# A twelve-unit ring for the expert weights, half of it over the front's dead temporaries, and a loop over pairs of items

## The reference, cut to what matters

```python
x = x + merged @ w_out[l]                       # end of the two attention branches
x = x + moe_ffn(rms_norm(x, ffn_norm_g[l]), router_w[l], router_b[l],
                w_gate_up[l], b_gate_up[l], w_down[l], b_down[l])
return rms_norm(x, final_norm_g)
...
top_logit, top_e = lax.top_k(logits, TOP_K)     # 4 of 32 experts for each token
gate = jax.nn.softmax(top_logit, axis=-1)
...
gu = xb @ w_gu[e] + b_gu[e]                     # 1024 x 2048 weights per expert
glu = jnp.minimum(gu[:, :D_FF], SWIGLU_LIMIT)
lin = jnp.clip(gu[:, D_FF:], -SWIGLU_LIMIT, SWIGLU_LIMIT)
act = glu * jax.nn.sigmoid(SWIGLU_ALPHA * glu) * (lin + 1.0)
return act @ w_d[e] + b_d[e]                    # 1024 x 1024 weights per expert
```

## Time and profile before

| | |
|---|---|
| median of 3 runs | 1183.23 us (1181.96 to 1184.37) |
| profiled execution, its own time | 1181.82 us |
| its span | 1180.0 us |
| granted TensorE clock, mean | 0.995 |
| TensorE busy | 1102.3 us, 93% |
| VectorE, ScalarE, GpSimd busy | 279.0, 164.0, 10.2 us |
| moved by DMA | 431.22 MB, 365 GB/s over the span |

### The profile page before, as it was taken

How to read it: one execution, slowest core, us unless ns; L and a number is a source line. 1 busy time by engine, 2 the same in 40 slices (tenths; PEclk the granted TensorE clock), 3 DMA queues, 4 the chain that set the end, 5 groups by cost and what they waited for, 6 DMA issues and landing times.

```text
span 1180.0 us, 13249 instructions
## 1 busy us (share of the span) xinstructions
PE 1102.3 (93%) x5094; PEld 473.9 (40%) x5094; DVE 279.0 (24%) x662; ACT 164.0 (14%) x341; POOL 10.2 (1%) x28
## 2 busy tenths in 40 slices
PE   7999999999999999999999999999999999999996
PEld 5578887633333333333333333333333333333332
DVE  2056432321111211111111111111111111111113
ACT  2144440210001000000000000000000000000002
POOL 0101000000000000000000000000000000000000
PEclk9999999999999999999999999999999999999998
DMA  9823313469999999999999999999999999999993
GB/s 307 315 75 147 136 72 126 160 288 405 429 429 430 427 427 430 429 428 427 429 429 429 427 427 430 429 428 427 429 429 430 427 427 430 429 428 427 429 429 158
DMA packets 43265, 431.22 MB, mean 365 GB/s; under 512 B 5808, under 2 KB 7984, under 8 KB 18640
## 3 DMA queue, kind: packets, MB, share of 16 engines
q1 hardware_dynamic: 42960, 430.46, 87.2%
q10 hardware_dynamic: 288, 0.52, 0.1%
HBM read 429.92 MB, written 1.05 MB: 365 GB/s over the span
## 4 chain that ended last, share of the span: by engine, by line
DMA 57%; PE 41%; DVE 1%; issue 1%; ACT 1%; SPq 0%; DVEq 0%; ACTq 0%
DMA raw<-in_w_gate_up 56%; PE bank L835 15%; PE bank L493 8%; PE bank L526 4%; PE bank L851 4%; PE bank L718 2%; PE bank L497 2%; PE bank L535 1%; PE bank L672 1%; PE bank L770 1%; PE bank L803 1%; DMA x_res<-in_x 1%; PE bank L736 0%; PE bank L813 0%; DVE x_res L1457 0%
## 5 line engine op out<-in xcount | busy, mean ns | idle before, releaser
L835 PE MATMUL bank<-raw,xT 128*64 128x512 f32 x2048 | 465.2, 598 | 56.0 <-DMA raw<-in_w_gate_up 54.4
L835 PEld LDWEIGHTS bank<-raw,xT 128*64 128x64 f32 x2048 | 137.9, 136 | 357.7 <-issue 230.7
L851 PE MATMUL bank<-raw,actT 128*64 128x512 f32 x1024 | 233.2, 597 | 0.0
L1408 DVE COPY ev_gu<-bank 128x512 f32<-128x512 f32 x32 | 22.1, 692 | 532.7 <-PE bank L835 532.7
L851 PEld LDWEIGHTS bank<-raw,actT 128*64 128x64 f32 x1024 | 71.7, 137 | 132.5 <-issue 126.7
L1401 DVE TENSOR_TENSOR gub<-bank,bias_gu 128x512 f32<-128x512 f32 x64 | 43.9, 686 | 169.5 <-PE bank L497 169.5
L1065 ACT COPY ev_gu<-bank 128x512 f32<-128x512 f32 x32 | 18.8, 586 | 413.3 <-PE bank L835 413.3
L803 PE MATMUL bank<-ev_dn,scat 64*128 64x512 f32 x256 | 64.3, 621 | 1.2 <-ACT ev_dn L1075 0.8
L770 PE MATMUL bank<-x_res,onehot 128*64 128x512 f32 x264 | 62.3, 592 | 0.0
L493 PE MATMUL bank<-hT,raw 128*128 128x256 f32 x256 | 58.9, 383 | 0.0
L493 PEld LDWEIGHTS bank<-hT,raw 128*128 128x128 f32 x256 | 47.5, 190 | 8.4 <-issue 2.5
(11 more groups left out here) (234 smaller groups left out, 594.1 us busy)
## 6 DMA issues: line engine op xcount, KB each, us to landing
raw<-in_w_gate_up SPq DMA_DIRECT2D x128, 2048.0 KB, 25.4
raw<-in_w_down SPq DMA_DIRECT2D x64, 2048.0 KB, 24.9
raw<-in_w_in SPq DMA_DIRECT2D x6, 2048.0 KB, 14.5
raw<-in_w_out SPq DMA_DIRECT2D x2, 2048.0 KB, 9.7
raw<-in_w_branch_mla SPq DMA_DIRECT2D x1, 2048.0 KB, 9.0
raw<-in_w_branch_dsa SPq DMA_DIRECT2D x1, 2048.0 KB, 7.8
raw<-in_w_in SPq DMA_DIRECT2D x1, 1664.0 KB, 16.8
x_res<-in_x SPq DMA_DIRECT2D x2, 512.0 KB, 4.9
```

Of the source, the lines that this page charges most:

```text
L835: mm = pe.matmul(GU[pair][half * SLOTS:(half + 1) * SLOTS, :], xT[:, c, b, :], w[:, at:at + BLK], start=u == 0 and k == 0, stop=last and k ...
L851: mm = pe.matmul(DN[half * SLOTS:(half + 1) * SLOTS, :], actT[:, c, u, :], w[:, at:at + BLK], start=u == 0 and c == 0, stop=u == DN_UNITS ...
L1408: dve.tensor_copy(ev_gu[:, 1, :], GU[1][:, :]).then_inc(lin_ev, 1)
```

## The change

The ring gets twelve slots (`SLOTS_W`). Six of them are those of the front, now called `front_raw`; the other six lie over the front's temporaries, which are laid out anew in six groups of 16 KB per partition. The expert units go round the twelve slots in the order `ORDER`, which begins with the slots whose contents are dead first. The first twelve units are issued one by one, each behind a wait for the last reader or writer of what lies there; from the thirteenth on the waits are on `used` again, twelve units back. Since twelve units are two items, the loops of SyncE and TensorE go over pairs of items (`pairs`); those of ScalarE and VectorE still go over items.

```diff
+SLOTS_W = 2 * UNITS
+ORDER = (6, 7, 1, 8, 2, 3, 4, 9, 10, 5, 0, 11)
...
-        raw = sb("raw", [P, RING, UNIT])
-        n_items = sb("n_items", [P, 1], I32)
+        n_items = sb("n_items", [P, 2], I32)
...
+        front_raw = fb("front_raw", [P, RING, UNIT])
...
+        raw = sb("raw", [P, SLOTS_W, UNIT])
-        ev_x = sb("ev_x", [P, BLK])
-        ev_dn = sb("ev_dn", [P, BLK])
+        ev = sb("ev", [P, BLK])
-        sig = sb("sig", [P, BLK])
-        scat = sb("scat", [P, TOKENS])
+        glu, lin, sig = gub[:, 0], gub[:, 1], ev_gu[:, 0]
+        scat = gated[:, :, :].rearrange("p t n -> p (t n)")
+        final_g = raw[:, ORDER[0], 0:D]
...
+        def landed_expert(eng, j, place):
+            slot = ORDER[place % SLOTS_W]
+            eng.wait_ge(raw_in[slot], 16 * j + (16 * (place // SLOTS_W + 1) + arrived(slot)))
+            return raw[:, slot, :]
...
@@ SyncE @@
-            sp.dma_start(cst[:, :], consts).then_inc(cst_in, 16)
+            sp.dma_start(cst[:, :], consts[:, 0:KEPT]).then_inc(cst_in, 16)
...
+            sp.dma_start(cst2[:, 0:sum(CONST.values()) - KEPT], consts[:, KEPT:]).then_inc(cst2_in, 16)
...
+            sp.wait_ge(ml_rot, 1)
+            load_gate_up(0, 0, ORDER[0])
+            sp.wait_ge(s_mx, 7)
+            sp.wait_ge(pv_ps, 6)
+            load_gate_up(0, 1, ORDER[1])
+            used_up(sp, 7)
+            load_gate_up(0, 2, ORDER[2])
+            sp.wait_ge(s_mx, 12)
+            load_gate_up(0, 3, ORDER[3])
+            used_up(sp, 8)
+            load_gate_up(1, 0, ORDER[4])
+            used_up(sp, 9)
+            load_gate_up(1, 1, ORDER[5])
+            used_up(sp, 10)
+            load_gate_up(1, 2, ORDER[6])
+            load_gate_up(1, 3, ORDER[7])
+            sp.wait_ge(br_ok, 2 * KC)
+            load_down(0, 0, ORDER[8])
+            used_up(sp, 11)
+            load_down(0, 1, ORDER[9])
+            used_up(sp, 12)
+            load_gate_up(2, 0, ORDER[10])
+            sp.wait_ge(lg_ps, 2)
+            load_gate_up(2, 1, ORDER[11])
...
+                def load(k, start, e, u):
+                    sp.wait_ge(used, SLOTS_W * j + (k + 1 - SLOTS_W))
+                    start(e, u, ORDER[k])
+                load(0, load_gate_up, even, 2)
+                load(1, load_gate_up, even, 3)
...
+            sp.wait_ge(used, SLOTS_W * pairs + (1 - SLOTS_W))
+            for n in range(2):
+                sp.dma_start(final_g[:, n * BLK:(n + 1) * BLK],
+                             final_norm_g[n * BLK:(n + 1) * BLK].partition_broadcast(P)).then_inc(final_in, 16)
@@ TensorE @@
-            with pe.Fori(2, items) as i:
-                gate_up(i, 0)
+            with pe.Fori(1, pairs) as j:
+                for odd in range(2):
+                    i = 2 * j + odd
+                    gate_up(j, odd, 0)
...
@@ ScalarE @@
             def glu_out(i):
                 act.wait_ge(glu_ps, i + 1)
+                if not isinstance(i, int) or i > 0:
+                    act.wait_ge(act_ok, i)
...
-            act.wait_ge(sums_ok, 1)
-            for j in range(2):
-                act.dma_start(gain[:, j * BLK:(j + 1) * BLK], ...
@@ VectorE @@
+            dve.wait_ge(cst2_in, 16)
...
+            dve.tensor_scalar(n_items[:, 0:1], r_s[:, 0, 0:1], float(EXPERTS - 2), None, ALU.add)
+            dve.tensor_scalar(n_items[:, 1:2], r_s[:, 0, 0:1], 0.5, float(EXPERTS // 2 - 2), ALU.mult, ALU.add).then_inc(n_ok, 1)
...
+            weigh_tokens(0)
             with dve.Fori(2, items) as i:
-                weigh_tokens(i - 2)
                 next_tokens(i)
                 activate(i)
                 product(i)
+                dve.wait_ge(scat_ps, 2 * i - 2)
+                weigh_tokens(i - 1)
@@ the program @@
-    nc = _bacc.Bacc("TRN2", target_bir_lowering=False, num_devices=1)
+    nc = _bacc.Bacc("TRN2", target_bir_lowering=False, num_devices=1, dynamic_dma_scratch_size=1024)
```

More of the change, by code:

```diff
@@ L62 @@
 GATES_ATT = (0, 1, 2, 3, 4, 5, 6, 7, 8, 9, 10)
-CONST = {"ident": P, "before": P, "ones": P, "slot": P, "causal": P, "invfreq": ROPE // 2}
+CONST = {"ident": P, "ones": P, "slot": P, "before": P, "causal": P, "invfreq": ROPE // 2}
 CONST_AT = {}
@@ L68 @@
     CONST_AT[_name] = sum(CONST[k] for k in CONST_AT)
+KEPT = CONST_AT["before"]
 def constants():
@@ L212, in build @@
         bd_in = sem("bd_in")
-        sums_ok = sem("sums_ok")
         final_in = sem("final_in")
-        raw_in = [sem(f"raw_in{i}") for i in range(RING)]
+        raw_in = [sem(f"raw_in{i}") for i in range(SLOTS_W)]
         out_done = sem("out_done")
@@ L467, in _ @@
-            sp.wait_ge(n_ok, 1)
-            items = sp.value_load(n_items[0:1, 0:1], min_val=EXPERTS - 2, max_val=EXPERTS * CHUNKS - 2) + 2
-            with sp.Fori(2, items) as i:
-                e = sp.snap(i % EXPERTS)
-                e_last = sp.snap((i + (EXPERTS - 1)) % EXPERTS)
-                for u in range(UNITS):
-                    sp.wait_ge(used, UNITS * i + (u + GU_UNITS - UNITS - RING + 1))
-                    if u < GU_UNITS:
-                        load_gate_up(e, u, slot_of(GU_UNITS + u))
-                    else:
-                        load_down(e_last, u - GU_UNITS, slot_of(GU_UNITS + u))
@@ L478, in _ @@
-            for u in range(DN_UNITS):
-                sp.wait_ge(used, UNITS * items + (u + GU_UNITS - UNITS - RING + 1))
-                load_down(EXPERTS - 1, u, slot_of(GU_UNITS + u))
+            sp.wait_ge(ml_rot, 1)
[7 more added lines that the diff above has]
+            load_gate_up(0, 3, ORDER[3])
@@ L802, in scatter @@
                         rows = slice(half * SLOTS, (half + 1) * SLOTS)
-                        mm = pe.matmul(ACC[2 * t + half][:, :], scat[rows, t * P:(t + 1) * P], ev_dn[rows, :],
+                        mm = pe.matmul(ACC[2 * t + half][:, :], scat[rows, t * P:(t + 1) * P], ev[rows, :],
                                        start=False, stop=True, skip_group_check=True)
@@ L839, in gate_up, with down @@
                 mm.then_inc(used, 1)
-            def down(i, u, place):
+            def down(j, odd, u, last=False):
+                i = 2 * j + odd
                 pe.wait_ge(act_ok, i + 1)
@@ L845, in down @@
                     pe.wait_ge(dn_ev, i)
-                landed_expert(pe, i + 1, place)
-                w = raw[:, slot_of(GU_UNITS + place), :]
+                w = landed_expert(pe, j, UNITS * odd + (GU_UNITS if last else UNITS + GU_UNITS - DN_UNITS) + u)
                 for c in range(4):
@@ L900, in _ @@
             scatter(items - 2)
-            down(items - 1, 0, 0)
+            down(pairs - 1, 1, 0, last=True)
             turn_scatter(items - 1)
-            down(items - 1, 1, 1)
+            down(pairs - 1, 1, 1, last=True)
             scatter(items - 1)
```

201 lines of the change are left out of this document (97 added, 104 removed).

## The result

The changed kernel takes 1148.88 us (median of 4 runs, 1144.81 to 1149.92), the kernel before 1183.8 us (median of 4, 1181.96 to 1187.07). The ratio is 0.9699, with a 95% interval of 0.9671 to 0.9727. The forecast was 1153.9 us with a range of 1151.0 to 1158.5 us: the direction and most of the size are right, and the time lies 2.1 us under the range. The profiled execution has a span of 1148.1 us against 1180.0 us.

What follows compares the result with a forecast made beforehand. Weight transfers were taken to bound the last stage, TensorE the stages before. Execution 1181.82 us less 29.4 us for six units' lead, other terms nothing, gives 1152.5; 1.4 us up to the median makes 1153.9 us, range 1151 to 1158.5.

Steps and rivals of the forecast that it cites:

- 4.894 us a unit: Last stage: time of one expert unit's transfer, at six units per 29.365 us item, in both kernels.
- the lead: Last stage: twelve slots put loads six units further ahead, so every arrival comes 29.4 us earlier.
- D. A deeper queue moves more per us: Rival on the weight stream: more transfers in flight raise the rate to 435 GB/s, giving 1141 us; 2%.
- The floor: Item loop: TensorE's free run ends at 1077.7 us, leaving 38.2 us of slack; transfers still bind from near 680 us.
- The end of item 31's gate and up matmuls: Sign near the loop's end: this point moves from 1145.29 us to near 1116 us.
- The twelve early issues: Front: twelve expert units issued ahead of 231.3 us as their slots come free, the last landed by 238 us.
- Shared buffers: Item loop: added waits on VectorE and ScalarE for merged buffers cost nothing, with 1.3 us per item as cover.
- The end: After the last item: the scatter matrix's wait and the later load of final gains cost nothing, with 4 us of cover.
- The start: Front: splitting the constants costs or gains at most 0.5 us, taken as 0.
- A, fewer units ahead: Rival on the loads: each unit too late to keep the queue full costs 4.9 us, 1158.8 us for one; 5%.
- B, code fetched at each jump: Rival in TensorE's loop: the doubled body is fetched anew, fifteen jumps at 4.8 us, giving 1188 us; 4%.
- C: Rival on the bound: transfers are hidden anyway and TensorE is the true bound, so time stays at 1183; 1%.

Runs made afterwards that it cites:

- e3_after_off_256: The changed kernel with 192 bytes of padding ahead of the ring, so its slots begin 192 past a multiple of 256: 1153.07 us, ratio 0.9733.
- six ahead: The changed kernel with its first twelve units loaded early, but later loads held to six units ahead of the one in use: 1172.89 us, ratio 0.9911.
- nine ahead: The changed kernel with its first twelve units loaded early, but later loads held to nine units ahead of the one in use: 1163.94 us, ratio 0.9821.
- half units: The changed kernel with each expert unit loaded and released in two halves of 1 MB, in rows of 8 KB: 1151.6 us, ratio 0.9723.
- kernel before on 256: The kernel before with 64 bytes of padding ahead of its ring, so its slots begin at a multiple of 256 bytes: 1177.96 us, ratio 0.9946.

## Why the prediction was wrong

Its mechanism was right and one term was mis-sized: **"4.894 us a unit", taken over for the changed kernel.** The prediction priced the lead (six units by 4.894 us, 29.4 us) and left the pitch of the stream at "29.365" in the last stage; a unit of the changed kernel took 4.863 us. The lead measured 29.3 us at the old place of the ring and 29.2 us at the new one. But the pitch became 29.176 us, worth 899.14 against 904.84 us in the kernel before, 5.7 us that stand in no term. The cause is where the ring begins: the new layout happens to start its slots at a multiple of 256 bytes of the partition, the old one 192 past it. It is shown from both sides: the kernel before gains 0.5% by 64 bytes of padding, and the changed kernel loses the fast pitch by 192 or by 128. The prediction looked at which buffers share a place and when each comes free, never at the address that comes out. The rival nearest to it in size, "*D. A deeper queue moves more per us*" (2%, 1141 us), had the sign and the wrong cause: a queue of six at the new place is fast, a queue of twelve at the old one slow.

**The sum against the traces.** The span fell by 31.9 us: 29.2 from the lead, 5.7 from the place of the ring, 1.7 at the end, less 2.4 for the clock's fall in item 1 and 2.2 by which the first expert matmul is later. Of what wasn't forecast, 5.7 us belongs to the change; the rest, 2.4 and 2.2 us lost and 1.7 us won, is TensorE's pace in the two executions compared: falls of the clock, but for 0.6 of the 2.2 us, which are lost at the front's start (below). Without them the change would stand at 34.9 us, further from the 29.4 us of the prediction, not nearer.

**The floor.** "The loop's last stage is still that of the transfers, entered ... near 680 us": TensorE was busy in all of 290 to 680 us and in 364.71 of 390 us from 720 us on. That the transfers bound the end is right. The place isn't: the gathers keep the pitch of 26.70 us to 708.38 us, an item later than forecast, because the transfers are now faster. With the ring at the old place it comes as forecast, at 679.96 us (first row the changed kernel, second `e3_after_off_256`):

```profile
708.38 1.89 PE L804 MATMUL bank<-x_res,onehot 128*64 128x512 f32 x8
```

```profile
679.96 1.89 PE L805 MATMUL bank<-x_res,onehot 128*64 128x512 f32 x8
```

The waits left are 25.9 us where 31 were forecast, for the same reason.

**The end of item 31's gate and up matmuls, "near 1116 us".** It stands at 1115.07 us. That is right only by the two errors that cancel: the faster stream, 5.7 us early, against the later start and the fall in item 1.

**The twelve early issues.** All within 0.7 us of the releases read from the earlier trace rows, and "a DMA rate above 300 GB/s in the slice from 206 to 236 us" came as 369 in the slice that begins at 201 us. The next one is at 263, as the queue is empty from about 239 us, when the twelfth unit has landed, until the loop's first release lets the next issue go at 246.4 us. The forecast had both ends of this gap, "landed by 238" and the issues from 243.8 us on; its 2 us of idle queue are those behind it.

**Shared buffers, forecast at nothing.** The scatter matrix on VectorE, which got the new wait, starts right behind the product ahead of it:

```profile
318.47 0.69 DVE L1456 TENSOR_TENSOR actT<-gub,ev_gu 128x512 f32<-128x512 f32 x1 [0.76 <-PE bank L881]
319.08 0.60 DVE L1399 TENSOR_SCALAR gated<-cst,posc,gates 128x128 f32<-128x128 f32 x2
```

No idle time is put down ahead of the second row, in which the wait would show. Right.

**The end, forecast at nothing.** The scatter matrix of the last item waits for the scatter before it, and TensorE turns it after the matmuls behind that scatter, as written:

```profile
1127.65 1.99 PE L837 MATMUL bank<-ev,gated 64*128 64x512 f32 x8 [0.46 <-ACT gated L1093]
...
1129.57 3.65 PE L881 MATMUL bank<-raw,actT 128*64 128x512 f32 x16
1129.82 0.60 DVE L1399 TENSOR_SCALAR gated<-cst,posc,gates 128x128 f32<-128x128 f32 x2 [3.12 <-PE bank L837]
...
1133.16 0.44 PE L530 MATMUL bank<-cst,gated 128*128 128x128 f32 x2
```

VectorE idles for 3.12 us, and TensorE's next matmuls begin without a gap. The final gains, 41.3 us from issue to landing, aren't waited for. That the end is 1.7 us shorter isn't the change's doing. The same scatter and the sixteen matmuls behind it took 2.71 and 4.58 us in the kernel before, where the granted clock was 0.90 from 1155 us and 0.76 from 1160 us; here they take 1.99 and 3.65 us at a full clock. That is the 1.65 us: a fall of the clock that the kernel before has there and this one hasn't.

**The start, "0.5 us either way; I take 0".** The split of the constants did what it should: TensorE's wait for `x` is 5.2 us instead of 5.7. The first expert matmul is nevertheless 2.2 us later, which lies outside my bounds. 1.6 us are the fall of the clock near 231 us. The other 0.6 us are lost in the front's first 64 matmuls, which begin at the same time in both and end later in the changed kernel:

```profile
12.09 21.07 PE L526 MATMUL bank<-raw,hT 128*128 128x200 f32 x64 [1.13 <-DVE hT L1142]
```

```profile
12.08 21.70 PE L559 MATMUL bank<-front_raw,hT 128*128 128x200 f32 x64 [1.13 <-DVE hT L1172]
```

In six ahead, with the same front, these 64 take 19.95 us. In the three traces of the changed kernel's code without the fall (six ahead, nine ahead, half units) the first expert matmul stands at 238.5 to 239.9 us. So neither part is the new code's own work.

**The rivals.** A, fewer units ahead, didn't occur; the price it was given is confirmed by nine ahead, 14.25 us for three. B, code fetched at each jump, didn't occur: 12 packets of code where there were 11, no gaps at every second item. The Trainium skill (Runtime: NRT & Kernel Launch, Instruction fetch mechanics) has both a window of 512 instructions and room for 2048 on TensorE. A body of 504 recorded matmuls and weight loads, with its waits, register operations and the branch besides, runs here 15 times without new code, which fits the second if each record is one instruction. C is excluded by the result.

## What to carry to other kernels

Where a queue of transfers ends last, a deeper ring gains the number of units that it adds to the lead, by the time of one unit. The lead has to be kept to the end, since an early load that is followed by later waits gives nearly all of it back. After any change of layout, look at the byte of the partition at which the destination of large transfers begins: 0.65% of the stream hung on 64 bytes of padding here, and the place can be read in advance from the list of buffers. Split transfers to release memory sooner only after pricing the smaller rows and transfers over the whole stream: here they cost 4.8 us more than they brought.

## What the runs showed of the hardware

- **Place of the destination.** Units of 2 MB in rows of 16 KB stream at 29.175 us per item of six when the slots begin at a multiple of 256 bytes of the partition (three places), and at 29.365 us when 128 or 192 past it (four places).
- **Size of row and transfer.** The same bytes in rows of 8 KB and transfers of 1 MB take 29.436 us per item, at a multiple of 256.
- **A long queue holds up its issuer.** With the twelve-slot ring SyncE's issues of gate and up weights take 4.0 us at the median between 720 and 1050 us, and up to 11.4 us, where the front's take 0.33 us. With nine units ahead they stay at 0.33 us (shortest, median and longest in ns; first the changed kernel, then nine ahead):

```profile
L436 SPq DMA_DIRECT2D raw<-in_w_gate_up x45: 332/3961/11411, 724.6 to 1049.2; - x45
```

```profile
L436 SPq DMA_DIRECT2D raw<-in_w_gate_up x46: 332/333/333, 722.4 to 1048.6; - x46
```

  Transfers then land 43 to 46 us after their issue (medians over the kernel). It costs nothing here, since the DMA share stays at 1.01 and SyncE has nothing else to do. But a small transfer behind the others waits as long: the final gains, two of 256 KB, land 41.3 us after their issue.
- **Falls of the clock in a busy stretch.** From 2.4 to 1.2 GHz for some 3.5 to 7 us, near 231 and 262 us and in the last item, each worth 1.6 to 2.4 us, in some traces and not in others. They aren't the change's own: the kernel before with only the reserved area cut has them at 231 and 262 us too. The one at 262 us begins ahead of the gap that stands there, and filling the gap didn't keep it away. A fall before or at the start of the stream moves everything behind it.

**Open.** What brings the falls. Ahead of the one near 262 us TensorE has eight matmuls of 32 partitions (L847, 3.70 us) and then transposes; whether the kind of matmul matters wasn't tried. Why the place of the slots costs 0.65%, and not the 1.6% that I estimated above. And why the ratios on the chips come out 1 to 2 us apart from what the traces' terms give, for the kernel before on 256 and for the changed one off it; the intervals, of some 2 us either way, nearly cover this, and the traces of both lack the fall in item 1, which is worth as much.
